# Expert stage: the down projection's context strips moved ahead of its full-width products

## What is computed

```python
gates, idx = lax.top_k(aff.T, cap)
xs = ht[idx]
a = jnp.einsum('ecd,edf->ecf', xs, w_gate)
u = jnp.einsum('ecd,edf->ecf', xs, w_up)
y = jnp.einsum('ecf,efd->ecd', jax.nn.silu(a) * u, w_down) * gates[..., None].astype(h.dtype)
out = jnp.zeros((t, d), h.dtype).at[idx.reshape(-1)].add(y.reshape(-1, d))
```

## Time and profile before

| | |
|---|---|
| median of 3 runs | 3174.97 us (3174.19 to 3179.51) |
| profiled execution | 3178.7 us |
| span of the profiled execution | 3176.0 us |
| mean granted clock of TensorE | 0.953 |
| PE busy | 2915.9 us, 92% |
| DVE busy | 1772.3 us, 56% |
| ACT busy | 1574.4 us, 50% |
| DMA, mean | 211 GB/s |

### The profile page before, as it was taken

One profiled execution on the slowest core, in us unless ns is written; L12 is line 12 of the kernel. 1 busy time (PEld: TensorE's weight loads), 2 busy tenths in 40 slices (PEclk: granted clock), 3 DMA queues, 4 the chain that ended last, 5 costly groups with the idle time before them and its releaser, 6 DMA issues. The chain is left out here.

```text
span 3176.0 us, 61303 instructions
## 1 busy us (share of the span) xinstructions
PE 2915.9 (92%) x23879; PEld 2200.5 (69%) x23879; DVE 1772.3 (56%) x2627; ACT 1574.4 (50%) x2473; POOL 435.5 (14%) x448
## 2 busy tenths in 40 slices
PE   5899998898399999999999999999999999999993
PEld 2799996587277767667676767667676767667772
DVE  2333331131667666666666666666666666666763
ACT  3322221133265656556565656556565656556652
POOL 3243331021201010101101010101101010101102
PEclk9999999898599999999999999999999999999996
DMA  9211102153577686868677686868678686868764
GB/s 385 76 41 35 34 17 78 50 175 119 196 238 253 232 293 218 295 228 270 229 262 261 229 290 210 295 232 272 230 256 266 229 291 205 295 234 274 249 237 147
DMA packets 483864, 668.99 MB, mean 211 GB/s; under 512 B 14689, under 2 KB 418993, under 8 KB 480562
## 3 DMA queue, kind: packets, MB, share of 16 engines
q1 hardware_dynamic: 476978, 644.45, 59.8%
q0 software_dynamic: 6656, 20.98, 2.6%
HBM read 633.39 MB, written 31.98 MB: 209 GB/s over the span
## 5 line engine op out<-in xcount | busy, mean ns | idle before, releaser
L1210 DVE TENSOR_TENSOR wGU_lo<-rawW,wGU_hi 128x1024 fp32r<-128x1024 f32 x700 | 824.9, 1218 | 74.3 <-ACT wGU_hi L1205 74.3
L1205 ACT ACTIVATE wGU_hi<-rawW 128x1024 fp32r<-128x1024 f32 x704 | 731.9, 1054 | 148.8 <-PE psGU L1420 139.7
L1420 PE MATMUL psGU<-wGU_hi,X_hi 128*128 128x512 f32 x1408 | 588.9, 418 | 54.4 <-issue 51.5
L1420 PE MATMUL psGU<-wGU_lo,X_hi 128*128 128x512 f32 x1408 | 568.4, 404 | 0.0
L1420 PE MATMUL psGU<-wGU_hi,X_lo 128*128 128x512 f32 x1408 | 567.7, 403 | 0.0
L1594 DVE TENSOR_TENSOR wD_lo<-rawW,wD_hi 128x1024 fp32r<-128x1024 f32 x352 | 415.2, 1220 | 63.1 <-ACT wD_hi L1527 63.1
L1586 DVE TENSOR_TENSOR hid_lo<-psT,hid_hi 128x256 fp32r<-128x256 f32 x176 | 74.5, 423 | 533.1 <-ACT hid_hi L1522 533.1
L1420 PEld LDWEIGHTS psGU<-wGU_hi,X_hi 128*128 128x128 f32 x1408 | 273.7, 194 | 124.5 <-issue 56.3
L1522 ACT ACTIVATE hid_hi<-psT 128x256 fp32r<-128x256 f32 x176 | 67.5, 384 | 576.6 <-PE psT L1464 576.2
L1527 ACT ACTIVATE wD_hi<-rawW 128x1024 fp32r<-128x1024 f32 x352 | 351.8, 1051 | 0.0
L1433 PE MATMUL psC<-rawW,Xc 128*32 128x128 f32 x11264 | 344.0, 274 | 0.0
(11 more groups left out here) (235 smaller groups left out, 3673.2 us busy)
## 6 DMA issues: line engine op xcount, KB each, us to landing
rawW<-in_w_gate SPq DMA_DIRECT2D x176, 1024.0 KB, 5.5
rawW<-in_w_up SPq DMA_DIRECT2D x176, 1024.0 KB, 8.1
rawW<-in_w_down SPq DMA_DIRECT2D x176, 1024.0 KB, 8.4
wm<-in_w_mod SPq DMA_DIRECT2D x24, 1024.0 KB, 8.6
raw<-in_w_in SPq DMA_DIRECT2D x32, 192.0 KB, 2.5
rawc<-catT SPq DMA_DIRECT2D x10, 512.0 KB, 6.0
acc<-x SPq DMA_DIRECT2D x10, 512.0 KB, 2.7
xn<-xn SPq DMA_DIRECT2D x10, 512.0 KB, 4.1
```

The lines of the kernel that those rows point to most:

```text
L1205: act.activation(hi, w, ACT.Copy).then_inc(f_whi, 1)
L1210: eng.tensor_tensor(lo, w, hi.bitcast(F32), ALU.subtract).then_inc(f_wlo, 1)
L1420: mm = pe.matmul(psGU[:].rearrange("p n f -> p (n f)"), X[a][:, k, :], wGU[b][:, k, :, :].rearrange("p n f -> p (n f)"), start=(k == 0 and ...
```

## The change

In `down` the block of strip products is moved ahead of the full-width products. Its waits go with it: the wait for hidc (f_hc), and a new wait, on PE itself, for the slot of raw down weights (`raw_ready`). The wait f_y for the expert before stands ahead of both; the waits f_hl and f_dlo stay with the full-width products. The last of these now raises f_d.

```diff
                     def down(e, i, first):
                         s = STEPS * e + i
-                        pe.wait_ge(f_hl, s + 1)
                         if i == 0 and not first:
                             pe.wait_ge(f_y, e)
+                        pe.wait_ge(f_hc, s + 1)
+                        raw_ready(pe, D_, e, i)
+                        for f in range(2):
+                            for half in range(2):
+                                at = (2 * f + half) * CP
+                                w = raw[:, i % RING, D_, f * D + half * 512:f * D + (half + 1) * 512]
+                                pe.matmul(psP[at:at + CP, :], hidc[:, f, :], w, start=(i == 0),
+                                          stop=(i == STEPS - 1), skip_group_check=True)
+                        pe.wait_ge(f_hl, s + 1)
                         for f in range(2):
                             pe.wait_ge(f_dlo, 2 * s + f + 1)
                             for a, b in ((0, 0), (0, 1), (1, 0)):
                                 for half in range(2):
-                                    pe.matmul(psS[:, half, :], hid[a][:, f, :], wD[b][:, f, half * 512:(half + 1) * 512],
-                                              start=(i == 0 and f == 0 and a == b),
-                                              stop=(i == STEPS - 1 and f == 1 and a == 1), skip_group_check=True)
-                        pe.wait_ge(f_hc, s + 1)
-                        for f in range(2):
-                            for half in range(2):
-                                at = (2 * f + half) * CP
-                                w = raw[:, i % RING, D_, f * D + half * 512:f * D + (half + 1) * 512]
-                                mm = pe.matmul(psP[at:at + CP, :], hidc[:, f, :], w, start=(i == 0),
-                                               stop=(i == STEPS - 1), skip_group_check=True)
+                                    mm = pe.matmul(psS[:, half, :], hid[a][:, f, :], wD[b][:, f, half * 512:(half + 1) * 512],
+                                                   start=(i == 0 and f == 0 and a == b),
+                                                   stop=(i == STEPS - 1 and f == 1 and a == 1), skip_group_check=True)
                         mm.then_inc(f_d, 1)
```

## The result

The changed kernel takes 3131.4 us at the median (3128.0 to 3135.5, 4 runs) against 3175.3 for the kernel before: a ratio of 0.986, 95% interval [0.985, 0.988], so 44 us faster. The forecast was 3112 with a range of 3083 to 3148. The profiled execution took 3131.95 us with a span of 3130.2, against 3178.7 and 3176.0.

A forecast was written before the change was run, and what follows sets the result against it. PE's queue was taken to bound the expert stage. Plain steps (43.7 us), loop boundaries (18.1) and the tail (1.3) summed to 63.1 us saved, giving 3112 us, range 3083 to 3148.

The forecast's parts named there:

- What bounds: Expert stage, 176 steps: PE's queue sets the pace; ScalarE waits 576.6 us for its transposes.
- C to P: Down context strips (P) follow gate/up context strips (C) like one more round, 1.77 us after their start: 0.12 us saved.
- S to T: Transposes (T) directly behind full-width down products (S), both of form 128*128: 0.09 us saved per step.
- T: Transposes of hf, then hfc: first load made ahead, 0.31 us to the hfc transpose instead of 0.37, 0.06 saved.
- The waits: Down context strips need hidc and the raw down slot earlier; 7 us of cover for hidc, costed at nothing.
- Loop boundaries: 13 jumps back of PE's expert loop: sequencer's queue lead brings branch 2.20 us after context strips' start; 1.39 us saved each.
- an unchanged idle time ahead of G: Sign of being wrong: PE's idle before gate/up products at boundaries should fall from some 3.9 to some 2.8 us.
- The rival of a shorter branch and a clock that holds: At 13 boundaries: branches 12 us shorter in all, half the slow-clock loss saved, 17 us; together 3083, chance 0.20.
- The rival in which the branch's time runs from the end of PE's work: Boundaries of PE's expert loop give only 0.27 us each; 3126 us, chance 0.17.
- Tail: Last down block: context strips fit into the wait for wD_lo, saving about 1.3 us.
- The sum: 176 down blocks: 162 plain at 0.27, 13 boundaries at 1.39, last 1.3; 63.1 us saved, to 3112.
- The slower rival: Clock falls in the longer run of strips, costing about 2.65 us per fall; 3229 at 44 steps, chance 0.03.

The follow-up runs named there:

- Experiment 3: Against the kernel before: only half the change, down context strips placed behind the transposes, not behind the gate/up context strips; 3153.6 us, ratio 0.995.
- experiment 2: Changed kernel with transposes of hfc and gathered context rows made full form (128 partitions, upper half zero); 3068.7 us, ratio 0.967 to the kernel before.
- experiment 1: Changed kernel with hfc made on DVE ahead of the step's last wGU_lo copy instead of behind it; 3099.9 us, ratio 0.977 to the kernel before.
- experiment 5: Changed kernel with one instruction per iteration of PE's expert loop announcing the closing branch's target; 3040.1 us, ratio 0.958 to the kernel before.

## Why the prediction came out as it did

The time fell into the range and on the forecast side, 19 us above the forecast: the plain steps came as forecast, the boundaries did not. Step by step:

- *What bounds.* Right: PE's queue set the pace; ACT's wait fell by 45.9 us.
- *C to P, S to T, T.* Right, and nearly to size: 1.77 us, no excess at S to T, 0.31 for T. Two first weight loads that were not made ahead (P's and T's) and two changes of form went, as worked out; P also took 0.97 instead of 0.99 to its successor, so a plain step gave 0.29 where the forecast had 0.27. The rule of the Trainium skill ("TensorE: Matmul & The Clock Gate", What overlaps and what doesn't, in Part 3), by which a weight load runs beside products only with another row group, would have had C to P pay; P's 1.77 is sixteen rounds of C and no more, so the measurement is against it here. Experiment 3 shows the prices edge by edge, and experiment 2 that forms cost without strips.
- *The waits.* Right: the new wait cost nothing. P came at 1.77 us after C in every step.
- *Loop boundaries.* Wrong, and the largest error: 18.1 us were forecast; the last steps lost 2.1 instead, and the steps behind them gave 3.4. The step that failed is the count by which the sequencer was 31 to 33 entries ahead and would reach the branch 2.20 us after C. What held it at the branch was the wait for hfc, as experiment 1 shows, and hfc kept its time. That the count came out alike in two places was chance: at T's register operation, the other place, it was not hfc that held the sequencer, since hfc ended 0.9 us later there, and after the change the same way of counting gives 40 issued and four started, 36 ahead. What sets the time of that operation is open. The branch stayed at 3.55 us after C, and as the rest of the step became 0.29 shorter, PE's idle time grew by as much, which takes back the saving of the 13 last steps; the 5.9 us on the page hold some 2 more, since the branches lasted 0.14 us longer in the mean. The prediction had named an unchanged idle time ahead of G as a sign of being wrong; it grew.
- *The rival of a shorter branch and a clock that holds* needed a branch that starts earlier, which the change did not bring. In experiment 1, which did, the branches were shorter and PE spent less time at the lower clock, as this rival had it; whether the earlier start is the cause was not shown.
- *The rival in which the branch's time runs from the end of PE's work* came nearer to the time, 3126, but for a wrong reason: experiment 1 moved the branch alone, and its time moved with it. The Trainium skill ("Runtime: NRT & Kernel Launch", Instruction fetch mechanics) says that a taken branch to a place no longer held forces a fetch before execution goes on; experiments 1 and 5, with 6.4 us from the branch on and 0.73 with the target told ahead, agree, and so does the packet of instructions under experiment 5.
- *Tail.* The mechanism was right, the size was off: 3.6 us instead of 1.3. P came out of the path behind S, as forecast, and S ran at 0.23 us a product instead of 0.43, because the granted clock was 1.00 and not 0.50. The forecast had no term for that, though the slow pairs stand in the earlier trace rows.
- *The sum.* 147 undisturbed steps gave 42.1, the boundaries 1.3, the tail 3.6, the rest took back 1.1: 45.8 us of the span. Forecast were 43.7 for 162 steps, 18.1 and 1.3. Without the boundary term the forecast would have been 3174.97 - 43.7 - 1.3 = 3130. That this comes so near is partly luck: 162 steps at 0.27 were counted where 147 gave 0.29, and the rest of the errors nearly cancel.
- *The slower rival* did not occur: inside an expert no pair of products ran at the slow pace.

## What to carry to other kernels

Products of one form belong together: each change between 128\*128, 128\*32 and 64\*128 cost PE about 0.1 us in this kernel (for the 64-row form it may be the form itself), and often a weight load of another 0.1 that was not made ahead, so count the changes per step. Where a loop's jump back is long, as PE's is here, its time runs from the moment the branch is reached, and that moment was set by the last wait ahead of it in program order (here for hfc, which DVE makes); look there before counting queue entries. Two places that agree on one number are no mechanism: look for the number in a place where the rival mechanism gives another one.

## What had not been expected of the hardware

The jump back of PE's loop lasts 5.6 to 7.7 us before and after the change, while ACT's and DVE's loops over the experts in the same trace jump in 0.04 to 0.06 and PE's own loop over the heads (L398) in 0.21 to 0.23; with the target told ahead it lasts 0.7 at the median. After idle times of 2.9 us and more at the boundaries the granted clock fell nearly everywhere, and the 24 products of G took up to 2.8 us more. At two of the 13 boundaries of experiment 1, with idle times of 3.3 us, it did not, though it did at others there after 3.2. What decided there was not tried.
